# Sample-state products of a hybrid decoder step: one half-precision pass over 96 stacked rows in place of a full-precision product over 32 rows

## What is computed

```
s_new = exp(b_last)[..., None] * s0 + einsum('bshk,bshv->bhkv', k * exp(b_last[:, None] - b), v)      # HGRN2
s_new = exp(c * log_gamma)[None, :, None, None] * s0 + einsum('bshk,bshv->bhkv', k * k_dec[None, :, :, None], v)   # retention
```

## Time and profile before

| | |
|---|---|
| median of 3 runs | 1771.18 us (1766.13 to 1771.87) |
| span of the profiled execution | 1765.4 us |
| PE busy | 1585.4 us, 90% of the span |
| DVE, ACT, POOL busy | 930.3, 657.9 and 154.2 us |
| mean granted TensorE clock | 0.930 |
| matmuls of the sample steps (L619) | 64 records, 39.6 us |

### The profile page before, as it was taken

How to read it: one execution, slowest core, us unless ns; L and a number is a source line. 1 busy time by engine, 2 the same in 40 slices (tenths; PEclk the granted TensorE clock), 3 DMA queues, 4 the chain that set the end, 5 groups by cost and what they waited for, 6 DMA issues and landing times.

```text
span 1765.4 us, 31743 instructions
## 1 busy us (share of the span) xinstructions
PE 1585.4 (90%) x12187; PEld 1263.6 (72%) x12187; DVE 930.3 (53%) x1493; ACT 657.9 (37%) x936; POOL 154.2 (9%) x126
## 2 busy tenths in 40 slices
PE   4699999998879999999957999999896999999994
PEld 3577777776658888878745777777674888887883
DVE  5766744443575555533266767444366555553334
ACT  3635423232263433422154544233235443333223
POOL 3111110000020000000030111100002000000002
PEclk8789889998989999999978989999987999999997
DMA  5121231220312233223321222222121323322321
GB/s 185 51 62 51 73 109 62 84 73 26 96 50 94 95 95 95 73 79 90 97 66 48 73 73 73 76 85 73 50 74 47 96 95 95 95 80 71 98 65 51
DMA packets 175036, 137.86 MB, mean 78 GB/s; under 512 B 5064, under 2 KB 169192, under 8 KB 174776
## 3 DMA queue, kind: packets, MB, share of 16 engines
q1 hardware_dynamic: 168192, 113.46, 21.1%
q0 software_dynamic: 5408, 18.60, 3.1%
q10 hardware_dynamic: 1372, 4.95, 0.8%
HBM read 124.91 MB, written 12.07 MB: 78 GB/s over the span
## 4 chain that ended last, share of the span: by engine, by line
PE 76%; DVE 10%; ACT 6%; issue 4%; DVEq 3%; ACTq 1%; DMA 1%; SPq 0%
PE ACC L506 60%; PE SCR L619 2%; PE SCR L536 2%; PE OT L627 2%; ACT WH L825 1%; PE SCR L657 1%; DVE X L1189 1%; PE OT L679 1%; DVE Z L1220 1%; PE OT L595 1%; DVE Fb L1202 1%; DVE WL L1149 1%; DVEq L1259 1%; PE SCR L722 1%; PE OT L594 1%
## 5 line engine op out<-in xcount | busy, mean ns | idle before, releaser
L506 PE MATMUL ACC<-XH,WH 128*128 128x280 f16 x2432 | 503.7, 290 | 74.7 <-DVE XL L1192 43.1
L506 PE MATMUL ACC<-XL,WH 128*128 128x280 f16 x2432 | 502.6, 289 | 0.0
L506 PE MATMUL ACC<-XH,WL 128*128 128x280 f16 x2432 | 502.2, 289 | 0.0
L506 PEld LDWEIGHTS ACC<-XH,WH 128*128 128x128 f16 x2432 | 237.4, 101 | 158.7 <-DVE XL L1192 45.9
L1149 DVE SCALAR_TENSOR_TENSOR WL<-stage,WH 128x2048 f16<-128x2048 f32 (+1 forms) x116 | 245.9, 2120 | 180.8 <-ACT WH L825 169.1
L506 PEld LDWEIGHTS ACC<-XL,WH 128*128 128x128 f16 x2432 | 243.4, 100 | 58.8
L506 PEld LDWEIGHTS ACC<-XH,WL 128*128 128x128 f16 x2432 | 243.5, 100 | 58.4
L825 ACT ACTIVATE WH<-stage 128x2048 f16<-128x2048 f32 (+1 forms) x116 | 204.8, 1765 | 103.0 <-PE ACC L506 85.7
L506 PE MATMUL ACC<-shared,WH 128*128 128x280 f16 x1408 | 225.4, 283 | 0.2
L506 PEld LDWEIGHTS ACC<-shared,WH 128*128 128x128 f16 x1408 | 137.6, 98 | 30.7 <-issue 0.8
L506 PE MATMUL ACC<-shared,WL 128*128 128x280 f16 x704 | 141.3, 283 | 0.0
(11 more groups left out here) (241 smaller groups left out, 1870.7 us busy)
## 6 DMA issues: line engine op xcount, KB each, us to landing
stage<-in_w_in_dram SPq DMA_DIRECT2D x64, 512.0 KB, 4.8
stage<-in_w_a_dram SPq DMA_DIRECT2D x44, 512.0 KB, 4.2
stage<-in_w_b_dram SPq DMA_DIRECT2D x44, 512.0 KB, 4.6
stage<-in_w_down_dram SPq DMA_DIRECT2D x32, 384.0 KB, 3.1
stage<-in_w_down_dram SPq DMA_DIRECT2D x32, 320.0 KB, 3.4
out_dram<-shared POOLq DMA_DIRECT2D x16, 512.0 KB, 3.4
stage<-in_w_o_dram SPq DMA_DIRECT2D x16, 512.0 KB, 3.9
shared<-in_state_hgrn_dram POOLq DMA_DIRECT2D x8, 512.0 KB, 5.8
```

The lines of the kernel that those rows point to most:

```text
L506: last = mm(ACC[:, acc, h, 0:HALF], lhs, x[:, xk + k, h * HALF:(h + 1) * HALF], start=begin, stop=end)
```

## The change

The sample keys and values are each brought into three copies of 32 rows. ACT writes two more copies of the sample columns of V (`twice(V)`), DVE two more of KE (`twice(KE)`), so that one transpose of 96 columns gives 96 rows. ACT rounds all 96 rows to f16 in KV3. DVE then replaces the third copy of the keys and the second copy of the values by what the rounding lost (`low_sample_rows`). One f16 matmul over 96 rows thus adds key high by value high, key high by value low, and key low by value high. The f32 values that the sample output needs are copied apart (VTS). The 0/1 table and the key decay are repeated over 96 rows, and VX is f16.

`scr_read[0]` of the transposes is now counted up by DVE, and POOL waits for `kv_low` in place of `tok_ready`.

```
-        VX = sb("VX", [TS, DEC_BATCH, P])
-        KVTS = sb("KVTS", [TS, 2, P])
+        VX = sb("VX", [TS3, DEC_BATCH, P], F16)
+        KV3 = sb("KV3", [TS3, 2, P], F16)
+        VTS = sb("VTS", [TS, P])
...
+        def twice(t):
+
+            return t[:, T:T + 2 * TS].rearrange("p (a t) -> p a t", a=2)
...
-                pool.wait_ge(tok_ready, hh + 1)
-                nc.gpsimd.tensor_tensor(VX[:, :, :], KVTS[:, 1:2, :].to_broadcast([TS, DEC_BATCH, P]), bcast(seqm[0:TS, :], P),
+                pool.wait_ge(kv_low, hh + 1)
+                nc.gpsimd.tensor_tensor(VX[:, :, :], KV3[:, 1:2, :].to_broadcast([TS3, DEC_BATCH, P]), bcast(seqm[0:TS3, :], P),
...
-                mm(SCR[:, bank, :], KVTS[:, 0, :], VX[:, 4 * n:4 * n + 4, :].rearrange("p b v -> p (b v)"),
+                mm(SCR[:, bank, :], KV3[:, 0, :], VX[:, 4 * n:4 * n + 4, :].rearrange("p b v -> p (b v)"),
...
-                mm(cols_, KVTS[:, 1, :], PTSS[:, :], start=True, stop=False, skip_group_check=True)
+                mm(cols_, VTS[:, :], PTSS[:, :], start=True, stop=False, skip_group_check=True)
...
+                if buf is V:
+                    last = f(twice(V), ACC[:, c, 1:2, HALF - TS:HALF].to_broadcast([P, 2, TS]), ACT.Copy, scale=INV_W)
...
-                f(KVTS[:, :, :], SCR[0:TS, 0, 0:2 * P].rearrange("p (n v) -> p n v", n=2), ACT.Copy).then_inc(scr_read[0], 1)
+                f(KV3[:, :, :], SCR[0:TS3, 0, 0:2 * P].rearrange("p (n v) -> p n v", n=2), ACT.Copy)
+                f(VTS[:, :], SCR[0:TS, 0, P:2 * P], ACT.Copy).then_inc(kv_high, 1)
...
-                f(KVTS[:, 0, :], SCR[0:TS, 0, 2 * P:3 * P], ACT.Copy, scale=tab[0:TS, ds(cols["k_dec_s"][0] + p, 1)])
-                f(KVTS[:, 1, :], SCR[0:TS, 0, 3 * P:4 * P], ACT.Copy).then_inc(scr_read[0], 1)
+                f(KV3[:, 0, :], SCR[0:TS3, 0, 2 * P:3 * P], ACT.Copy, scale=tab[0:TS3, ds(cols["k_dec_s"][0] + p, 1)])
+                f(KV3[:, 1, :], SCR[0:TS3, 0, 3 * P:4 * P], ACT.Copy)
+                f(VTS[:, :], SCR[0:TS, 0, 3 * P:4 * P], ACT.Copy).then_inc(kv_high, 1)
...
+            def low_sample_rows(hh, at, decay):
+
+                keys, values = (slice(2 * TS, TS3), KV3[2 * TS:TS3, 0, :]), (slice(TS, 2 * TS), KV3[TS:2 * TS, 1, :])
+                dve.wait_ge(kv_high, hh + 1)
+                if decay is None:
+                    tt(keys[1], SCR[keys[0], 0, at:at + P], keys[1], ALU.subtract)
+                else:
+                    stt(out=keys[1], in0=SCR[keys[0], 0, at:at + P], scalar=tab[keys[0], ds(cols["k_dec_s"][0] + decay, 1)],
+                        in1=keys[1], op0=ALU.mult, op1=ALU.subtract)
+                tt(values[1], SCR[values[0], 0, at + P:at + 2 * P], values[1], ALU.subtract).then_inc(scr_read[0], 1)
+                dve.drain().then_inc(kv_low, 1)
...
+                nc.vector.tensor_copy(twice(KE), KE[:, TP:T].unsqueeze(1).to_broadcast([P, 2, TS]))
                 dve.drain().then_inc(ew_ready, 1)
...
                 for job in RT_JOBS:
+                    if job is RT_JOBS[1]:
+                        low_sample_rows(hh, 2 * P, p)
```

More of the change, by code:

```diff
@@ L46 @@
 T = TP + TS
+TS3 = 3 * TS
 HALF = T // 2
@@ L214, in hybrid_decoder_step @@
         Fb, T1, T2, T3, B, Q, QS, QD, KE, E, V, G = (
-            sb(n, [P, T + 2]) for n in ("Fb", "T1", "T2", "T3", "B", "Q", "QS", "QD", "KE", "E", "V", "G"))
+            sb(n, [P, T + (2 * TS if n in ("KE", "V") else 2)]) for n in ("Fb", "T1", "T2", "T3", "B", "Q", "QS", "QD", "KE", "E", "V", "G"))
         at = [0]
@@ L571, in transposes @@
                         for i, src in enumerate(sources):
-                            last = nc.tensor.transpose(SCR[0:TS, bank, i * P:(i + 1) * P], src[:, TP:T], ident)
+                            last = nc.tensor.transpose(SCR[0:TS3, bank, i * P:(i + 1) * P], src[:, TP:TP + TS3], ident)
                     last.then_inc(scr_full, 1)
@@ L648, in rest_transposes @@
                         nc.tensor.transpose(SCR[0:TAIL, 0, n * P:(n + 1) * P], src[:, 4 * P:TP], ident)
-                        last = nc.tensor.transpose(SCR[0:TS, 0, (2 + n) * P:(3 + n) * P], src[:, TP:T], ident)
+                        last = nc.tensor.transpose(SCR[0:TS3, 0, (2 + n) * P:(3 + n) * P], src[:, TP:TP + TS3], ident)
                     last.then_inc(scr_full, 1)
@@ L860, in read_acc @@
                 act.wait_ge(acc_full, 1 + tile + 1)
-                f(halves(buf[:, 0:T]), ACC[:, c, :, 0:HALF], ACT.Copy, scale=INV_W).then_inc(acc_read[c], 1)
+                last = f(halves(buf[:, 0:T]), ACC[:, c, :, 0:HALF], ACT.Copy, scale=INV_W)
+                if buf is V:
+                    last = f(twice(V), ACC[:, c, 1:2, HALF - TS:HALF].to_broadcast([P, 2, TS]), ACT.Copy, scale=INV_W)
+                last.then_inc(acc_read[c], 1)
                 if done is not None:
@@ L1199, in hg_gate @@
                 dve.drain().then_inc(f_ready, 1)
+                if low_rows is not None:
+                    low_rows()
                 dve.wait_ge(lnf_parts, n + 1)
@@ L1439, in group @@
                 split_lo(1, j)
+                hgrn_rows = (lambda: low_sample_rows(hh - 1, 0, None)) if steps else None
                 if kind == 0:
-                    hg_gate(l, head, tile)
+                    hg_gate(l, head, tile, hgrn_rows)
                     hg_exponents(l, head)
@@ L1449, in group @@
                     if after_hgrn:
+                        hgrn_rows()
                         dve.wait_ge(tok_ready, hh)
```

7 lines of the change are left out of this document (4 added, 3 removed).

## The result

| | before | changed |
|---|---|---|
| median | 1770.20 us (1766.13 to 1771.87, 4 runs) | 1745.04 us (1743.76 to 1746.22, 4 runs) |
| span of the profiled execution | 1765.4 us | 1744.2 us |
| PE busy | 1585.4 us | 1550.2 us |
| span less PE busy | 180.0 us | 194.0 us |
| mean granted clock | 0.930 | 0.933 |

The ratio is 0.9865, 95% interval 0.9849 to 0.9881. The gain is 25.2 us in the medians and 21.2 us in the profiled spans.

A forecast was written before the change was run, and what follows sets the result against it. TensorE held 76% of the chain and the changed product 2%, so at most about 37 us. Gross 23.4 less 6.9, 5.6 and 1.0 left 9.9 us: 1771.2 - 9.9 = 1761 us, range 1749 to 1772.

The forecast's parts named there:

- I take 1.9: HGRN2 loop heads with the product at half clock, three of six: 1.9 us saved each, between 1.2 and 3.
- the sum: Whole kernel: 23.4 us gross saving less 6.9, 5.6 and 1.0 us for what is added, net 9.9 us.
- the slow stretches shorten: Rival: HGRN2 heads leave 1.2 GHz some 3.5 us earlier, 1.7 us more each for six heads, 1751; chance 0.15.
- 23.4: Gross saving in us from the shorter product, over all retention and HGRN2 heads.
- the bank-0 wait: HGRN2 loop heads: the second product waits until DVE has read bank 0, so 0.9 us saved and not 1.6.
- The 0.23 us a pass: The changed product: one f16 pass of 512 columns costs 0.23 us at the fast clock, upper bound 0.5.
- 6.9 + 5.6 + 1.0: Added us: wait ahead of retention's second scores 6.9, POOL and DVE delay in HGRN2 5.6, small copies 1.0.
- POOL and DVE: HGRN2 heads: VX starts later, L1202 and L1203 wait for POOL; path 0.7 us longer a head, 5.6 us in all.
- The rule of the Trainium skill: Whoever issues first blocks the shared SBUF port pair; with queued L419 first, delay 0.85 us, 1.2 more over eight heads.
- POOL slow in f16: Rival: VX in f16 takes longer on POOL; at twice the time it costs 15 us, 1776; chance 0.10.
- 5.8 above the profiled span: Reference: median of the runs taken as 5.8 us above the profiled span, so 1771.2 - 9.9 = 1761 us.
- the 0.70 for "faster": Chance given to a kernel faster by over 0.3%, under 1765.9 us.

The follow-up runs named there:

- e11_fill_before: The kernel before with 22 extra, never read products ahead of each HGRN2 head's sample-state products: 1749.54 us, ratio 0.9882.
- e13_before_pool: The kernel before with POOL decaying the old states ahead of VX, product untouched: 1742.34 us, ratio 0.9840.
- e6_hg_x4: The changed kernel with each half-precision product issued four times in HGRN2 heads, once in retention heads: 1765.87 us, ratio 0.9982.
- e2_f16_x4: The changed kernel with each half-precision product issued four times in all heads: 1780.52 us, ratio 1.0083.
- e1_f32_96: The changed kernel with VX and KV3 in f32, all added copies and waits kept: 1779.03 us, ratio 1.0074.
- e3_f16_32: The changed kernel cut to one half-precision pass over 32 rows, without low parts or their added copies: 1742.20 us, ratio 0.9868.
- e17_f16_32_pool: One half-precision pass over 32 rows without low parts, plus POOL decaying the old states ahead of VX: 1731.09 us, ratio 0.9788.
- e15_before_pool2: The kernel before with POOL decaying the old states ahead of VX, run again in a second session: 1747.69 us, ratio 0.9882.

## Why the prediction was wrong

**The step that failed** is the size of the slow clock's term: "I take 1.9" for the HGRN2 heads with a slow product. In the three loop heads with a long slow stretch the sum held 1.0 us for the clock (1.9 - 0.9), in the two last heads 0.3 (1.9 less two products of 0.8 at full clock): 3.6 us in all. Measured, it is 12.8 us. The rows had the size in them: 9.6 us at 0.50 in one head, 3.7 us at 0.54 in its neighbour. I took a value between a stretch that ends at its own time (1.2 us) and one that ends sooner (3 us), and both were too small: a loop group with a long stretch went from 13.2 to 4.8 us of slow busy time, 4.2 us for the clock, where even the 3 us held only 2.1 for it. The prediction doesn't compare the lengths of the groups: two groups with the same instructions differed by 4.6 us, and in the clock alone. That slow time goes when the wait ahead of the product is filled or shortened is shown by e11_fill_before and e13_before_pool; that it comes back in part when the product is made long again, by e6_hg_x4. The rival "the slow stretches shorten" had the right mechanism, and a chance of 0.15. Its clock, 3.6 + 10.2 = 13.8 us, is close to the 12.8; that the sum comes out is in part luck, since it had 1.7 us in each of six heads and the time came from three, with some from the last HGRN2 head of layer 0.

**The other terms, point by point.**
- *Work.* At full clock the sum had 24.0 us: 23.4, less the 3.6 of the clock, plus 6 x 0.7 that the bank-0 wait takes back. Measured 22.5. Right. The 0.23 us a pass stands against 20.5 us of work at full clock for the 96 extra passes of e2_f16_x4, 0.21 each.
- *Idle time.* Waits 6.9 + 5.6 + 1.0 and the bank-0 wait of 4.2: 17.7 us. Measured 14.1 in the spans. In e1_f32_96, whose long product covers the bank-0 wait, it is 15.3 against 13.5. Right to 2 to 4 us. The 44.2 us of the earlier trace rows, which I had read as PE's idle time, are matmuls and weight loads together; the matmuls waited 19.2. Ahead of the product the wait grew by 10.4 us, where the sum had 5.6 + 4.2. Ahead of the retention scores it is 7.1 us (0.72 in a loop head where I had 0.8, 1.2 in the last), against 6.9, and the matmuls had no such wait before.
- *POOL and DVE.* The place was right; the mechanism was wrong in one point. I had L1202 (now L1228) get a turn between POOL's two operations, and L1203 (now L1229) wait for the stretched second, 0.7 us a head. It got none: it took 2.83 us and ended 0.6 us after L426. From the sample copy to the start of L1203 4.77 us passed (150.45 to 155.22), to that of L1229 5.56 us (146.82 to 152.38): 0.8 us more. The rule of the Trainium skill (SBUF — State Buffer, Who interferes with whom) that I had set aside, read so that the queued operation comes first, gave 0.85; here the trace agrees with that reading. The turns of the earlier trace rows hold for that stretch of the norm and not for this one; why, no run here shows.
- *POOL slow in f16.* VX takes 1887 ns, and took 1886. That rival falls.
- *The reference.* I set the sum against a median "5.8 above the profiled span". The changed kernel's profiled execution took 1745.75 us for a span of 1744.2, 1.5 us more. By that the profiled execution of before was at about 1767 us (an estimate), and some 4 us of the 16 us miss are the difference between one execution and the median. The rest is 9.2 us of the clock, 2.1 us of work and waits, and 0.7 us between the changed kernel's profiled execution and its median.

The sum without the clock was 6.3 us (24.0 - 17.7), measured 8.4 us. So the 0.70 for "faster" stood on terms that hold; but of the 21.2 us by which the profiled span fell, more than half is the clock's, for which the sum had 3.6. And that part is not the product's own: with POOL's order alike the clock gives nothing (it costs 1.2 and 12.0 us more in the two pairs of profiles), and the 5.7 and 9.3 us of work less waits don't show in the medians. In the kernel before, the long slow stretches were in three of the six HGRN2 loop groups (10.2 us and another 3.4), and in the last HGRN2 group of layer 0 (two of 6.8 us).

**What stays open.** What makes the clock stay down for 10 to 14 us in one group and 3.4 in the next is not settled. Groups with identical rows differ (48.4 and 43.8 us before; layers 0 and 1 in e3_f16_32; one group of six in e17_f16_32_pool), and a longer wait in the changed kernel went with shorter stretches, so neither the wait nor the product alone decides it. The two profiles of the same kernel in e13_before_pool and e15_before_pool2 are 9.1 us apart (1746.8 and 1737.7), and their second HGRN2 groups 2.4 us (46.03 and 43.61). Which of two such patterns an execution gets I can't tell beforehand. An order of the added copies that would shorten the wait ahead of the retention scores (e9_early_rows) has no measurement.

## What to carry to other kernels

Cut the trace into its repeated groups and print length and granted clock of each. Where equal groups differ in length and only the clock differs, that difference (here 4.6 us in 48) is the first thing to price and to try for by itself, before a product is rewritten: a swap of two GpSimd instructions gave about as much as the whole change (28.6 and 22.9 us in two sessions, and 25.2). Price an edit near such a place three times, in work at full clock, in idle time, and in busy time at the lower clock, and let the range take in the case in which all long slow stretches go. And compare a kernel that looks faster against the old one with the same cheap fix; the gain may not be its own.
